# Two output panels of the first layer as seven half-size products each, with a longer six-slot stretch of the weight ring

## The chip, the cores and the metric

One core of one Trainium2 chip runs the whole program. The metric is the device time of that core in microseconds (us); lower is better. A profile is one execution, recorded from the first to the last instruction (its span).

## The reference, cut to what matters

A float32 model on 256 tokens of width 1024: two blocks of attention with a convolutional feed-forward network, then two layers (`for i in range(DEPTH)`) of the part that matters here. Its first layer works on 512 tokens (256 of x and 256 of a context), its last one on the 256 of x.

```python
def branch_merge(ya, yb, yc, gates, w_branch, w_out):
    ga, gb, gc = jnp.split(jax.nn.sigmoid(gates), N_BRANCH, axis=-1)
    m = ga * (ya @ w_branch[0]) + gb * (yb @ w_branch[1]) + gc * (yc @ w_branch[2])
    return m @ w_out
...
        x = x + gt1 * branch_merge(ya, yb, yc, gates, w_branch[i], w_out[i])
...
            xc = xc + gt1c * branch_merge(yac, ybc, ycc, gatesc, w_branch[i], w_out[i])
        h2 = modulate(rmsnorm(x, g_norm2[i]), sh2, sc2)
        x = x + gt2 * ec_moe(h2, w_router[i], w_e1[i], w_e3[i], w_e2[i])
```

`ec_moe` sends each token through a router and then 16 experts, each with three matrices of 1024 x 1024 (4 MB each). All weights are read from HBM once, 664 MB in all.

## The kernel before, in words

**Tiling.** Activations are kept transposed: feature on the 128 partitions, token along the row. A weight panel is 512 output columns of a matrix, two chunks of 1 MB (512 rows x 512 columns each); `w_branch` has one chunk to a panel. `tiles_T` (L530) multiplies a panel directly: four tiles of 128 outputs, each with 8 matmuls (4 for `w_branch`) over all 512 tokens. Each float32 matmul stands as two records in the trace, so a direct panel of the first layer is 64 records of 512 columns. The sum of a tile lies in one of eight PSUM banks; VectorE (DVE) or ScalarE (ACT) empties it, and TensorE (PE) waits for a bank only when it comes round again (`Banks`).

**Half-size products.** `products` (L579) multiplies a panel by 512 tokens in another way: the panel and the tokens are cut in halves along rows, columns and tokens, and seven products p1 to p7 of half-size blocks take the place of eight. Each product is 8 matmuls (16 records) of 256 tokens. DVE forms three sums of token halves (T1_H, T2_H, T4_H, in `half_tokens`) and a fourth in place (`context_half`) once for all panels that share their tokens, and for each panel four sums of weight blocks (`prepare`: part 0 makes three, part 1 the fourth). PE waits for part 0 ahead of p6 and for part 1 ahead of p3. ACT copies p6 and p2 out of PSUM (`product_copy`), DVE adds the other five to them (`assemble`). The first layer's gate panels are already done so; the output panels (`w_out`) are direct.

**Order at the end of the first layer's mixing.** PE: gate panel (7 products), `w_branch` (direct), last gate panel, last `w_branch`, `shift_rows` (4 small matmuls), two direct output panels with `turn_tokens_half(0)` (16 transposes) after their fifth tile, the router's matmul (L1188), `turn_tokens_half(1)`, the router's steps between PE, ACT and DVE with three panels of modulation weights (`w_ada`, `ada_part`, L704), the gathering of tokens (L1235) and the experts (L1285). DVE: `merge_tile` (L2047, with one addition over four tiles, L2057, after each panel), then `add_gated` (L1736), which adds gate times output to the residual X.

**The ring.** One queue, SyncE's (SP), loads all chunks in the order in which PE uses them, into a ring of nine slots of 1 MB. The sums of tokens and weights lie in the last three (6 to 8). So `weight_chunks` marks stretches (`narrow`) in which only slots 0 to 5 may be used, and `slot_plan` gives each chunk the slot used longest ago among those allowed. A chunk waits at the head of the queue until its slot's last chunk has been used; one that takes back a slot of the sums waits for the last product of the stretch (`sums_done`, L1378). All behind it waits too.

**Loads aside.** Nine expert chunks of the first layer go to dead parts of the arena and of H, not to the ring: five when the attention is done, three when the gates are done, one when the output panels are done. `early` says ahead of which chunk of the queue each group is issued.

**The last layer's start.** PE: a panel for U (direct), two `ada_part`, a panel for V (two tiles, L571), two folds (L720), four transposes (L993), then products. DVE: four copies of U, two copies of V, `half_tokens`, `context_half`, `prepare` parts 0 and 1.

Of the kernel before, what the change touches and what calls it, by code (L numbers as in the profile page):

```python
# [21 lines left out]
KT = D // P  # L22
S = 256
# [156 lines left out]
def weight_chunks(a):  # L180
# [93 lines left out]
def build(nc, a, out, dump=None, stop=None):  # L274
    from contextlib import ExitStack
    ctx = ExitStack()
    with ctx:
# [175 lines left out]
        KT3, QT3, V3 = UT, VG, TG  # L453
        YCU = Y2[2]
        MBS = (view(0, 8, 512), view(0, 8, S))
        GS = [view(o, 4, 512) for o in (12288, 18432)]
# [51 lines left out]
        def _(pe):  # L508
# [69 lines left out]

            def products(rows=False):  # L579

# [3 lines left out]
                def product(name):  # L584
                    if name == PRODUCTS[0]:
# [5 lines left out]
                        panel.update(p1=(low[:, :, 0:S], H[:, 0:4, 0:S]), p2=(high[:, :, 0:S], H[:, 4:8, 0:S]),  # L591
                                     p3=(S4_W, H[:, 4:8, S:2 * S]), p4=(high[:, :, S:2 * S], T4_H),
                                     p5=(low[:, :, S:2 * S], T1_H), p6=(S2_W, T2_H), p7=(S3_W, H[:, 0:4, S:2 * S]))
                    if name in ("p6", "p3"):
                        pe.wait_ge(sums_ready.sem, sums_ready.nth("pe"))
                    w, t = panel[name]
                    o = banks.open("a" if name in ("p6", "p2") else "v")
# [6 lines left out]
                    ins.then_inc(banks.filled, 1)  # L604
                    turned_panels[-1][3][name] = sum(r[-1] == "a" for r in banks.uses)
                    if name in ("p5", "p4"):
# [3 lines left out]

                return [lambda name=name: product(name) for name in PRODUCTS]

# [345 lines left out]
            for i in range(DEPTH):  # L958
# [151 lines left out]

                def read_by(who):
                    return sum(r[-1] == who for r in banks.uses)

                def turn_mods():
# [59 lines left out]
                for f, step in enumerate(out_tiles):  # L1174
                    step()
                    written.append(read_by("v"))
                    if f == 4:
                        pe.wait_ge(banks.freed["v"], written[3])
                        turn_tokens_half(0)
# [4 lines left out]
                for s in range(qtiles // 2):  # L1184
                    for k in range(KT):
                        if s == 0 and (k % 4 == 0 or k == KT - 1):
                            pe.wait_ge(banks.freed["v"], written[min(k + 3, KT - 2) if k < KT - 1 else k])
                        ins = mm(o[32 * (k % 4):32 * (k % 4) + 32, s * S:(s + 1) * S], WRS[:, s, k, :], X[:, k, s * S:(s + 1) * S],  # L1188
# [208 lines left out]
        def _(v):  # L1397
# [375 lines left out]
            def context_half():  # L1773

                ve.tensor_tensor(H[:, 0:4, S:2 * S], H[:, 4:8, S:2 * S], H[:, 0:4, S:2 * S], ALU.subtract
                                 ).then_inc(half_sums.sem, half_sums.up())

            def part_of(dst, rows, f, t):

# [38 lines left out]
            for i in range(DEPTH):  # L1818
# [241 lines left out]
                def gate_sums(n):  # L2060

                    def last_part():
                        assemble("p4", GS[n % 2], more=n < 5)
# [3 lines left out]
                    return [lambda name=name: assemble(name, GS[n % 2], more=n < 5) for name in PRODUCTS[:-1]] + [last_part]  # L2067

# [32 lines left out]
                for half in range(2):  # L2101
                    if half and not last:
                        for step in gate_sums(5):
                            step()
                    for f in range(4):
                        merge_tile(4 + half, f)
                    stamp().then_inc(merged_ready.sem, merged_ready.up())
                o = banks.take("v")
# [3 lines left out]
                add_gated(i, 0, ns)  # L2112
                v.wait_ge(ssq_ready.sem, ssq_ready.nth("v"))
# [155 lines left out]
        def _(sc):  # L2269
# [179 lines left out]
            for i in range(DEPTH):  # L2449
# [138 lines left out]
                else:  # L2588
# [3 lines left out]
                    gate(GS[1])  # L2592
                table(LOG_EXP)

                def token_squares(t, half, o):
# [166 lines left out]
```

## Time and profile before

| | us |
|---|---|
| median of 3 runs | 2804.08 (2800.76 to 2805.63) |
| the profiled execution's own time | 2802.52 |
| its span | 2800.7 |
| PE busy in the span | 2551.8 (91%) |
| DVE busy | 948.9 (34%) |
| ACT busy | 464.7 (17%) |
| mean granted TensorE clock | 0.952 of full |

In a row of the trace, "1369.80 15.86 PE L550 ... x32 [5.19 <-DMA ring]" reads: 32 instructions of line 550 start at 1369.80 us, are over 15.86 us later, and PE had been idle for 5.19 us before them, until a transfer into `ring` landed. PEld is the loading of PE's stationary operand, SPq the DMA queue of SP, with the time at which a transfer was issued. The granted clock is 1.00 at 2.4 GHz and 0.50 at 1.2 GHz. Matmul records overlap, so the pace of a group is its time over its count.

### The profile page before, as it was taken

The numbers are of one execution on the slowest core, as the hardware profiler recorded it, in microseconds if no ns is written. First come the engines' busy times: TensorE is split into PE (matmuls) and PEld (weight loads), VectorE is DVE, ScalarE is ACT, GpSimd is POOL, SyncE is SP. The second block draws the span as 40 slices with busy tenths as digits, with TensorE's granted clock in tenths as the row PEclk, the third lists the DMA queues.
The fourth block names the chain that finished last, engine by engine and source line by source line (L and its number), as shares of the span: only waits on it lengthen the run. The fifth ranks groups of instructions, "written<-read, shape, count | busy, mean of one in ns | idle before, by whom it ended". The sixth has DMA issues, their size and how long they took to land.

```text
span 2800.7 us, 33063 instructions
## 1 busy us (share of the span) xinstructions
PE 2551.8 (91%) x14215; PEld 1721.2 (61%) x14215; DVE 948.9 (34%) x1929; ACT 464.7 (17%) x1019; POOL 60.5 (2%) x91
## 2 busy tenths in 40 slices
PE   8999999999999999999999998888999998666675
PEld 5678888568887877767554343334688885332322
DVE  2535501345514876554221121111574322110101
ACT  1320001141102132232021111113121211100001
POOL 1010000000000100000000000000100000000000
PEclk9999999999999999999999999999999999777767
DMA  8676444384444311210569999999414378999997
GB/s 306 221 191 179 156 155 155 120 271 150 151 150 138 113 61 61 75 61 31 195 241 378 414 421 421 421 421 346 128 61 166 105 287 341 421 421 421 420 421 293
DMA packets 202981, 664.42 MB, mean 237 GB/s; under 512 B 14226, under 2 KB 60596, under 8 KB 153940
## 3 DMA queue, kind: packets, MB, share of 16 engines
q1 hardware_dynamic: 193952, 641.97, 59.9%
q0 software_dynamic: 8688, 20.28, 2.8%
q8 instruction: 113, 1.85, 0.3%
q14 instruction: 32, 0.26, 0.0%
q10 hardware_dynamic: 196, 0.06, 0.0%
HBM read 661.12 MB, written 9.57 MB: 239 GB/s over the span
## 4 chain that ended last, share of the span: by engine, by line
PE 74%; DMA 21%; DVE 3%; ACT 2%; issue 1%; ACTq 0%; DVEq 0%
PE ps L550 29%; DMA ring<-in_w_e 20%; PE ps L603 15%; PE ps L1285 9%; PE ps L812 5%; PE ps L571 3%; PE ps L1262 1%; PE ps L1235 1%; PE ps L784 1%; PE ps L704 1%; PE ps L1084 1%; PE ps L1036 1%; PE ps L1049 1%; PE ps L1106 1%; PE ps L1024 1%
## 5 line engine op out<-in xcount | busy, mean ns | idle before, releaser
L1285 PE MATMUL ps<-ring,arena 128*32 128x256 f32 (+1 forms) x4344 | 588.1, 527 | 179.0 <-DMA ring<-in_w_e 171.3
L550 PE MATMUL ps<-normed,ring 128*128 128x256 f32 x2624 | 580.6, 382 | 5.1 <-ACT normed L2323 2.5
L550 PEld LDWEIGHTS ps<-normed,ring 128*128 128x128 f32 x2624 | 498.9, 191 | 80.2 <-ACT normed L2323 5.5
L1285 PEld LDWEIGHTS ps<-ring,arena 128*32 128x32 f32 (+1 forms) x4344 | 193.8, 133 | 553.1 <-DMA ring<-in_w_e 259.6
L550 PE MATMUL ps<-arena,ring 128*128 128x256 f32 (+1 forms) x832 | 255.8, 465 | 6.5 <-DMA ring<-in_w_branch 5.2
L550 PEld LDWEIGHTS ps<-arena,ring 128*128 128x128 f32 x832 | 156.8, 191 | 93.9 <-issue 73.3
L603 PE MATMUL ps<-ring 128*128 128x256 f32 x816 | 186.3, 382 | 2.7 <-DVE ring L1752 2.7
L603 PEld LDWEIGHTS ps<-ring 128*128 128x128 f32 x816 | 155.1, 192 | 27.3 <-issue 6.7
L603 PE MATMUL ps<-normed,ring 128*128 128x256 f32 x768 | 171.6, 380 | 0.1
L603 PEld LDWEIGHTS ps<-normed,ring 128*128 128x128 f32 x768 | 144.4, 190 | 21.3 <-issue 1.7
L812 PE MATMUL ps<-arena,ring 128*128 128x256 f32 x704 | 152.3, 379 | 0.0
L812 PEld LDWEIGHTS ps<-arena,ring 128*128 128x128 f32 x704 | 133.8, 190 | 18.2
L2231 DVE SCALAR_TENSOR_TENSOR arena<-arena,ps 128x512 f32<-128x512 f32 (+1 forms) x32 | 17.7, 554 | 366.6 <-ACT arena L2642 366.6
L1500 DVE TENSOR_TENSOR arena<-ps,small 128x256 f32<-128x256 f32 x128 | 52.0, 423 | 258.3 <-PE ps L550 209.7
L2650 ACT ACTIVATE normed<-ps 32x256 f32<-32x256 f32 (+1 forms) x96 | 42.7, 445 | 533.1 <-PE ps L1285 532.3
L1736 DVE SCALAR_TENSOR_TENSOR residual<-ps,small,residual 128x256 f32<-128x256 f32 x120 | 53.0, 481 | 186.4 <-PE ps L1262 115.1
L2236 DVE SCALAR_TENSOR_TENSOR arena<-arena,ps 128x512 f32<-128x512 f32 (+1 forms) x32 | 17.7, 554 | 233.1 <-PE ps L1285 233.1
L2345 ACT ACTIVATE arena<-arena 128x512 f32<-128x512 f32 (+2 forms) x32 | 31.2, 976 | 391.0 <-DVE arena L1581 267.4
L1494 DVE COPY arena<-ps 128x256 f32<-128x256 f32 (+1 forms) x58 | 25.9, 450 | 200.9 <-PE ps L812 129.7
L571 PE MATMUL ps<-ring,normed 128*128 128x512 f32 x192 | 83.7, 594 | 0.0
L2423 ACT ACTIVATE arena<-arena,small 128x512 f32<-128x512 f32 (+3 forms) x64 | 43.1, 674 | 236.6 <-DVE small L1706 124.2
L603 PE MATMUL ps<-ring,normed 128*128 128x256 f32 x320 | 71.4, 379 | 0.0
(288 smaller groups left out, 2229.4 us busy)
## 6 DMA issues: line engine op xcount, KB each, us to landing
ring<-in_w_e SPq DMA_DIRECT2D x363, 1024.0 KB, 20.3
ring<-in_w_in SPq DMA_DIRECT2D x56, 1024.0 KB, 5.3
ring<-in_w_ada SPq DMA_DIRECT2D x48, 1024.0 KB, 7.7
ring<-in_ffn_w_up SPq DMA_DIRECT2D x88, 512.0 KB, 6.4
ring<-in_ffn_w_down SPq DMA_DIRECT2D x22, 1024.0 KB, 5.4
ring<-in_dil_w_qkv SPq DMA_DIRECT2D x18, 1024.0 KB, 5.0
arena<-in_w_e SPq DMA_DIRECT2D x16, 1024.0 KB, 14.0
ring<-in_sb_w_qkv SPq DMA_DIRECT2D x12, 1024.0 KB, 14.9
```

The lines of the kernel that those rows point to most:

```text
L550: ins = mm(o[:, 0:n], slots[k // 4][:, k % 4, f * P:(f + 1) * P], src[:, k, 0:n], start=k == 0, stop=k == kts - 1)
L571: ins = mm(o, src[:, k, t * P:(t + 1) * P], slots[k // 4][:, k % 4, :], start=k == 0, stop=k == KT - 1)
L603: ins = mm(o[:, j * S:(j + 1) * S], still[:, k, j * P:(j + 1) * P], moving[:, k, :], start=k == 0, stop=k == 3)
L704: ins = mm(o[32 * (k % 4):32 * (k % 4) + 32, :], silu_pad[:, k, :], slots[k // 4][:, k % 4, :], start=k < 4, stop=k >= 4)
L784: ins = mm(outs[f][:, t:t + S], slots[k // 4][:, k % 4, f * P:(f + 1) * P], H[:, k, t:t + S], start=k == 0, stop=k == KT - 1)
L812: ins = mm(outs[f][:, 0:S], slot[:, k, f * P:(f + 1) * P], HID[:, 2 * j + k, :], start=j == 0 and k == 0, stop=j == FT // 2 - 1 and k == 1)
L1285: ins = mm(o[w * g:w * g + w, 0:cols], lhs(2 * c + j), part, start=c == 0 and j == 0, stop=c == KT // 2 - 1 and j == 1)
L1500: ve.tensor_tensor(dst, o[:, 0:S], rstd[:, 0:S], ALU.mult).then_inc(banks.freed["v"], banks.free("v"))
L1736: ins = ve.scalar_tensor_tensor(X[:, f, t], o[:, t], gt[:, f, s:s + 1], X[:, f, t], ALU.mult, ALU.add)
L2345: se.activation(x, x if src is None else src, ACT.Tanh, scale=scale).then_inc(gate_exp.sem, gate_exp.up())
L2423: return se.activation(s, s if src is None else src, ACT.Exp, bias=nmax[:, n % 2, k:k + 1], scale=scale, accum_out=ssum[:, n % 2, k:k + 1])
L2650: ins = se.activation(YE[q][r:r + CAP, (e - 1) // 4, g * cols:(g + 1) * cols], o[g * w + q * CAP:g * w + (q + 1) * CAP, 0:cols], ACT.Copy)
```

## The change

1. The two output panels of the first layer become seven products each, in the order p1, p2, p6, p7, p5, p3, p4, with sums of the merged tokens (`merged_sums`: four DVE subtractions). DVE adds each product straight to the residual (`add_products`), over two scratch areas to which ACT copies p2 and p6. The last output tiles' waits of the router's matmul are moved with it, and it takes the context half first.
2. `prepare` for the first output panel runs inside the last gate panel, for the second inside the first output panel.
3. The first layer's six-slot stretch ends behind the router's modulation panels instead of inside the last gates (chunks are numbered in the order of use: it ended at 165, now at 176). The eight loads aside go together ahead of chunk 170.
4. In the last layer, `half_tokens` and `context_half` come before the two copies of V instead of behind them.

```diff
+OUT_PRODUCTS = ("p1", "p2", "p6", "p7", "p5", "p3", "p4")
@@ weight_chunks
                 panel(w, 8 * BRANCH + b * D + half * BRANCH)
-                if i == 0 and b == MERGE_ORDER[2] and half:
-                    narrow[i] = (narrow[i], len(out))
                 panel(a["w_branch_2"][i][b], half * BRANCH, BRANCH)
         for half in range(2):
             panel(a["w_out_2"][i], half * BRANCH)
         ada_panels(ADA_ROUTER[i])
+        if i == 0:
+            narrow[i] = (narrow[i], len(out))
...
-        early[gates + 11], early[gates + 13] = held[:ASIDE_FIRST[i]], held[ASIDE_FIRST[i]:then]
+        if i == 0:
+            early[gates + 10] = held[:then]
+        else:
+            early[gates + 11], early[gates + 13] = held[:ASIDE_FIRST[i]], held[ASIDE_FIRST[i]:then]
@@ build, tensor
                 else:
                     gemm_products()
-                    sums_done.append(state["summed"])
...
-                out_tiles = tiles_T(MBS[i], qtok, halves=merged_ready) + tiles_T(MBS[i], qtok)
+                    out_products = (products(src=MBS[i], order=OUT_PRODUCTS,
+                                             before={"p1": merged_ready, "p2": merged_ready, "p6": half_sums, "p7": half_sums, "p4": half_sums})
+                                    + products(src=MBS[i], order=OUT_PRODUCTS))
+                    for n, step in enumerate(out_products):
+                        step()
+                        written.append(read_by("v"))
+                        if n == 9:
+                            pe.wait_ge(banks.freed["v"], written[6])
+                            turn_tokens_half(0)
+                    sums_done.append(state["summed"])
+                    x_written = {(1, 0): written[12], (0, 6): written[13]}
@@ build, vector
+            def merged_sums(part):
+                m = MBS[0]
+                if part == 0:
+                    ve.tensor_tensor(T1_H, m[:, 0:4, S:2 * S], m[:, 0:4, 0:S], ALU.subtract).then_inc(v_step.sem, v_step.up())
+                    return
+                v.wait_ge(v_step.sem, v_step.made)
+                ve.tensor_tensor(T2_H, m[:, 4:8, S:2 * S], T1_H, ALU.subtract).then_inc(half_sums.sem, half_sums.up())
+                ve.tensor_tensor(m[:, 0:4, S:2 * S], m[:, 4:8, S:2 * S], m[:, 0:4, S:2 * S], ALU.subtract
+                                 ).then_inc(half_sums.sem, half_sums.up())
+                v.wait_ge(half_sums.sem, half_sums.made)
+                ve.tensor_tensor(T4_H, T2_H, m[:, 4:8, 0:S], ALU.subtract).then_inc(half_sums.sem, half_sums.up())
...
+                o = product("p1")
+                v.wait_ge(banks.freed["a"], turned_panels[panels_read[0]][3]["p6"])
+                ve.tensor_tensor(c11, c11, o, ALU.add).then_inc(v_step.sem, v_step.up())
+                ve.tensor_tensor(c12, c12, o, ALU.add).then_inc(banks.freed["v"], banks.free("v"))
+                v.wait_ge(v_step.sem, v_step.made)
+                add(0, 0, c11)
+                o = product("p7")
...
                 if last:
+                    half_tokens(i)
+                    context_half()
                     for t in range(qtiles):
                         evac(VG[:, t, :], 512)
-                    half_tokens(i)
-                    context_half()
```

In `add_products` each `add` is two operations of the form of L1736 (128x256); p1 has two additions of 128x512 and one `add`, p7 one addition, `prepare(0, 1)` and one `add`, p5 two additions and two `add`, p3 one `add` and `prepare(1, 1)`, p4 one `add`. The second panel has no `prepare`.

## Rows read from the trace of the kernel before

**Rows 1.** The page: busy shares, and DMA's share of 40 slices of the span.

```profile
PE 2551.8 (91%) x14215; PEld 1721.2 (61%) x14215; DVE 948.9 (34%) x1929; ACT 464.7 (17%) x1019; POOL 60.5 (2%) x91
...
DMA  8676444384444311210569999999414378999997
```

**Rows 2.** Chain that ended last, 1300 to 2350 us: start, duration, what, instructions.

```profile
1326.70 13.73 PE ps L550 x32
1340.43 24.19 PE ps L603 x112
1364.64 5.11 DMA ring<-in_w_branch
1369.80 15.86 PE ps L550 x32
1386.00 34.43 PE ps L550 x80
...
1422.18 20.60 PE ps L550 x48
...
1885.39 20.32 DMA ring<-in_w_e
```

**Rows 3.** SP's queue in order of time: the first layer's output and router loads.

```profile
1364.64 0.37 SPq L1389 DMA_DIRECT2D ring<-in_w_branch  x1
1365.05 3.67 SPq L1389 DMA_DIRECT2D ring<-in_w_out  x4
```

**Rows 4.** Stretches: busy by engine, clock, DMA share, GB/s.

```profile
1360.00:1365.00 5.00, 4.61 (x22) 3.71 (x20) 1.04 (x2) 0.00 (x0) 0.00 (x0) 1.00 0.00 0
1370.00:1380.00 10.00, 10.00 (x20) 4.35 (x21) 1.38 (x2) 0.00 (x0) 0.00 (x0) 0.82 1.05 388
1470.00:1475.00 5.00, 3.54 (x26) 2.48 (x26) 4.05 (x12) 0.00 (x0) 0.00 (x0) 1.00 0.01 3
1700.00:1800.00 100.00, 89.74 (x428) 36.35 (x428) 17.20 (x39) 11.70 (x20) 0.00 (x0) 1.00 1.01 421
```

**Rows 5.** PE in order of time: third modulation panel, start of the first layer's experts.

```profile
1454.33 1.92 PE L704 MATMUL ps<-ring,small 128*32 128x512 f32 x16
...
1473.51 13.95 PE L1285 MATMUL ps<-ring,arena 128*64 128x512 f32 x64 [1.46 <-DVE arena L2201]
```

**Rows 6.** Groups by line and shape, 1298 to 1443 us.

```profile
L1736 DVE SCALAR_TENSOR_TENSOR residual<-ps,small,residual 128x256 f32<-128x256 f32 x15 | 6.6, 479 | 47.7 <-PE ps L550 47.7
L1792 DVE TENSOR_TENSOR arena<-arena,ps 128x512 f32<-128x512 f32 x2 | 1.4, 690 | 12.3 <-PE ps L603 12.3
L1748 DVE TENSOR_TENSOR ring<-ring 128x1024 f32<-128x1024 f32 x1 | 1.2, 1218 | 0.0
L2473 ACT ACTIVATE arena<-ps 128x512 f32<-128x512 f32 x4 | 2.4, 597 | 36.1 <-PE ps L603 36.1
```

**Rows 7.** DVE in order of time: the last merge of the first layer.

```profile
1385.69 0.69 DVE L2047 SCALAR_TENSOR_TENSOR arena<-arena,ps 128x512 f32<-128x512 f32 x1 [2.75 <-PE ps L550]
1386.41 2.29 DVE L2057 TENSOR_TENSOR arena<-arena 128x2048 f32<-128x2048 f32 x1
```

**Rows 8.** PE, then DVE, in order of time: the last layer's start.

```profile
1977.98 1.87 PE L720 MATMUL ps<-constants,arena 128*128 128x32 f32 x16
1983.77 1.09 PE L993 MATMUL ps<-constants,arena 128*128 128x128 f32 x4 [3.92 <-DVE normed L1775]
1987.57 5.57 PE L603 MATMUL ps<-ring 128*128 128x256 f32 x16 [2.72 <-DVE ring L1752]
2003.34 3.62 PE L603 MATMUL ps<-ring 128*128 128x256 f32 x16
...
1978.80 1.22 DVE L1767 TENSOR_TENSOR ring<-normed 128x1024 f32<-128x1024 f32 x1
1983.58 1.22 DVE L1748 TENSOR_TENSOR ring<-ring 128x1024 f32<-128x1024 f32 x1
```

**Rows 9.** Stretch at the start of the last layer, columns as in rows 4.

```profile
1980.00:1985.00 5.00, 1.09 (x4) 0.71 (x4) 4.90 (x6) 0.00 (x0) 0.00 (x0) 0.61 1.02 389
```

More of the change, by code:

```diff
@@ L454, in build @@
         YCU = Y2[2]
+        OUT_SUMS = (view(6144, 4, 512), view(18432, 4, 512))
         MBS = (view(0, 8, 512), view(0, 8, S))
@@ L577, in tiles_N, with read_by, products @@
                 return [lambda t=t: tile(t) for t in range(tiles)]
-            def products(rows=False):
+            def read_by(who):
+                return sum(r[-1] == who for r in banks.uses)
+            def products(rows=False, src=H, order=PRODUCTS, before={}):
                 panel = {}
                 def product(name):
-                    if name == PRODUCTS[0]:
+                    if name == order[0]:
                         taken = next_chunks(2)
@@ L604, in product @@
                     ins.then_inc(banks.filled, 1)
-                    turned_panels[-1][3][name] = sum(r[-1] == "a" for r in banks.uses)
+                    turned_panels[-1][3][name] = read_by("a")
                     if name in ("p5", "p4"):
@@ L609, in product @@
                         state["summed"] = len(banks.uses)
-                return [lambda name=name: product(name) for name in PRODUCTS]
+                return [lambda name=name: product(name) for name in order]
             def gemm_products(rows=False):
@@ L1109, in _ @@
                 staged(len(items), (0, da_scores), (2 * LAG, da_pv), (LAG, da_turn), fill=merge_tiles[gate_steps:])
-                def read_by(who):
-                    return sum(r[-1] == who for r in banks.uses)
                 def turn_mods():
@@ L1171, in _ @@
                 shift_rows()
-                out_tiles = tiles_T(MBS[i], qtok, halves=merged_ready) + tiles_T(MBS[i], qtok)
                 written = []
[L1174 to L1179, printed above, removed]
+                if last:
+                    out_tiles = tiles_T(MBS[i], qtok, halves=merged_ready) + tiles_T(MBS[i], qtok)
+                    for f, step in enumerate(out_tiles):
+                        step()
+                        written.append(read_by("v"))
+                        if f == 4:
+                            pe.wait_ge(banks.freed["v"], written[3])
+                            turn_tokens_half(0)
+                    x_written = {(0, 0): written[3], (0, 4): written[6], (0, 7): written[7]}
+                else:
+                    out_products = (products(src=MBS[i], order=OUT_PRODUCTS,
+                                             before={"p1": merged_ready, "p2": merged_ready, "p6": half_sums, "p7": half_sums, "p4": half_sums})
+                                    + products(src=MBS[i], order=OUT_PRODUCTS))
+                    for n, step in enumerate(out_products):
+                        step()
+                        written.append(read_by("v"))
+                        if n == 9:
+                            pe.wait_ge(banks.freed["v"], written[6])
+                            turn_tokens_half(0)
+                    sums_done.append(state["summed"])
+                    x_written = {(1, 0): written[12], (0, 6): written[13]}
                 out_done.append(len(banks.uses))
@@ L1183, in _ @@
                 pe.wait_ge(*banks.due)
-                for s in range(qtiles // 2):
+                for s in reversed(range(qtiles // 2)):
                     for k in range(KT):
-                        if s == 0 and (k % 4 == 0 or k == KT - 1):
-                            pe.wait_ge(banks.freed["v"], written[min(k + 3, KT - 2) if k < KT - 1 else k])
+                        if (s, k) in x_written:
+                            pe.wait_ge(banks.freed["v"], x_written[s, k])
                         ins = mm(o[32 * (k % 4):32 * (k % 4) + 32, s * S:(s + 1) * S], WRS[:, s, k, :], X[:, k, s * S:(s + 1) * S],
@@ new lines, in add_products, with add, product @@
+            def add_products(panel, more):
+                dst, f0 = OUT_SUMS[panel], 4 * panel
+                c11, c12, c21, c22 = (part_of(dst, False, f, t) for f in (0, 1) for t in (0, 1))
+                gt = mods[0][:, 16:24, :]
+                def add(f, t, src, g=gt):
+                    for j in range(2):
+                        n = f0 + 2 * f + j
+                        x = X[:, n, t * S:(t + 1) * S]
+                        ins = ve.scalar_tensor_tensor(x, src[:, j, :], g[:, n, t:t + 1], x, ALU.mult, ALU.add)
+                    return ins
+                def product(name):
+                    o = banks.take("v").rearrange("p (j n) -> p j n", j=2)
+                    v.wait_ge(banks.filled, banks.at["v"])
+                    return o
+                o = product("p1")
[5 more added lines that the diff above has]
+                o = product("p7")
+                v.wait_ge(banks.freed["v"], banks.frees["v"])
+                ve.tensor_tensor(c21, c12, o, ALU.add).then_inc(banks.freed["v"], banks.free("v"))
+                if more:
+                    prepare(0, 1)
+                v.wait_ge(banks.freed["v"], banks.frees["v"])
+                add(1, 0, c21).then_inc(v_step.sem, v_step.up())
+                o = product("p5")
+                ve.tensor_tensor(c22, c21, o, ALU.add).then_inc(v_step.sem, v_step.up())
+                ve.tensor_tensor(c12, c12, o, ALU.add).then_inc(banks.freed["v"], banks.free("v"))
+                v.wait_ge(v_step.sem, v_step.made)
+                add(1, 1, c22)
+                v.wait_ge(banks.freed["v"], banks.frees["v"])
+                add(0, 1, c12).then_inc(v_step.sem, v_step.up())
+                o = product("p3")
+                v.wait_ge(v_step.sem, v_step.made)
+                add(0, 1, o).then_inc(banks.freed["v"], banks.free("v"))
+                if more:
+                    prepare(1, 1)
+                o = product("p4")
+                add(1, 0, o, ampl).then_inc(banks.freed["v"], banks.free("v"))
+                panels_read[0] += 1
@@ L2062, in last_part @@
                     def last_part():
-                        assemble("p4", GS[n % 2], more=n < 5)
+                        assemble("p4", GS[n % 2])
                         v.wait_ge(banks.freed["v"], banks.frees["v"])
                         stamp().then_inc(gate_ready.sem, gate_ready.up())
-                    return [lambda name=name: assemble(name, GS[n % 2], more=n < 5) for name in PRODUCTS[:-1]] + [last_part]
+                    return [lambda name=name: assemble(name, GS[n % 2]) for name in PRODUCTS[:-1]] + [last_part]
                 gate_turn = [lambda: None] * 4
@@ L2104, in _ @@
                             step()
+                        merged_sums(0)
+                        ve.tensor_scalar(ampl, mods[0][:, 16:24, :], -1.0, None, ALU.mult).then_inc(v_step.sem, v_step.up())
                     for f in range(4):
@@ L2107, in _ @@
                     stamp().then_inc(merged_ready.sem, merged_ready.up())
+                    if not last and half:
+                        merged_sums(1)
                 o = banks.take("v")
@@ L2111, in _ @@
                                ).then_inc(banks.freed["v"], banks.free("v"))
-                add_gated(i, 0, ns)
+                if last:
+                    add_gated(i, 0, ns)
+                else:
+                    add_products(0, True)
+                    add_products(1, False)
+                    v.wait_ge(banks.freed["v"], banks.frees["v"])
                 v.wait_ge(ssq_ready.sem, ssq_ready.nth("v"))
@@ L2593, in _ @@
                 table(LOG_EXP)
+                if not last:
+                    for dst in OUT_SUMS:
+                        for name in ("p2", "p6"):
+                            product_copy(name, dst)
                 def token_squares(t, half, o):
```

8 lines of the change are left out of this document (5 added, 3 removed).

## The prediction

> **What bounds the kernel now.** I read the page first. PE is busy 91% of the span [rows 1], so a change that takes matmuls away can be worth their time, if PE is what sets the end where they stand. DMA's line has two stretches of nines: the experts of the two layers. There the chain of waits is made of transfers: each expert of the first layer ends in a wait like the 20.32 us one at 1885.39 [rows 2], while DMA runs at share 1.01 and 421 GB/s [rows 4]. So three kinds of stretch have to be told apart: where PE has work without a gap (the mixing), where DMA does (the experts), and the joint between them.
>
> The second view is the chain around the change [rows 2]. A gate panel of seven products is 24.19 us for 112 records, 3.46 us to a product. Then PE waits 5.11 us for the last `w_branch` chunk, and the two output panels take 34.43 + 20.60 = 55.03 us for 128 records. The queue says why it waits: that chunk is issued at 1364.64, when the last gate product ends, with all output chunks behind it [rows 3], and DMA had been idle until then (share 0.00 from 1360 to 1365, [rows 4]). It is a wait for a slot, not for bandwidth. It costs twice: the clock is at a mean of 0.82 from 1370 to 1380 [rows 4], and the `w_branch` panel behind the gap takes 15.86 us where its like took 13.73 [rows 2].
>
> The third is the joint. The first expert matmul starts at 1473.51 and was released by DVE, not by a transfer [rows 5]; DMA stands still from 1470 to 1475 (share 0.01, [rows 4]). So the ring is full before PE starts on the experts, and the stream of transfers restarts with the first chunk that PE frees. After that it is saturated, and what is left to move is the same. The experts of the first layer thus end earlier by as much as PE starts them earlier. All behind them follows from there, since the last layer's mixing follows PE too.
>
> **Part 1, the ring.** By the slot rule chunk 165 (the last `w_branch`) was the first to take back a slot of the sums, with 166 and 167. Now it takes the slot of chunk 159, used before the last two gate panels. PE goes on at 1340.43 + 24.19 = 1364.62. Gone are 5.11 us of waiting and 15.86 - 13.73 = 2.13 us of slow clock: **7.2 us**. What is late next? Chunk 167 waits for p4 of the gate panel before the last, done by 1326.70; with 5.1 us from issue to landing (1364.64 to 1369.80, [rows 2, 3]) it is there at 1332, and `prepare` for the first output panel wants it after p7 of the last gate panel, at 1354. Chunk 169 waits for p5 of that panel (1340.43 + 5 x 3.46 = 1357.7), lands at 1363, and is wanted at 1392. Both have over 20 us to spare. The eight loads aside are issued from 1358 and 1365, 8 x 2.5 us (1.05 MB at 421 GB/s) at the soonest; nothing wants them before the experts. Modulation chunks 170 to 173 wait for slots that come free by the end of the first output panel. Chunk 175 waits for the last output product; the third modulation panel is used 1454.33 - 1442.78 = 11.6 us after that [rows 2, 5], against 5.1 us of landing. SP has only this queue; POOL's is not touched.
>
> **Part 2, the products.** 2 x 24.19 = 48.4 us take the place of 55.03: **6.6 us** less. What they need beside PE: (a) DVE's four token sums, 4 x 1.22 = 4.9 us (form of L1748, [rows 6]). The first stands in the last gate panel's shadow. The merge ends at 1386.41 + 2.29 = 1388.70, 3.0 us after the last `w_branch` tile (1369.80 + 15.86 = 1385.66) [rows 2, 7], and a stamp more. The new order needs it for p2 only, which starts 0.34 us (`shift_rows`, 1385.66 to 1386.00) + 3.46 us behind that tile: covered, by some 0.6 us. This is the thinnest cover in the change; without it, it costs what it is short. The other sums are ready 4.4, 5.6 and 6.9 us behind the tile, p6, p7 and p4 start at 7.3, 10.7 and 24.5. (b) DVE's work on a panel: additions of 0.69, pairs of residual additions of 2 x 0.48 [rows 6]; p1 2.3, p7 1.7, p5 3.3, p3 and p4 1.0 each, with `prepare` 4.9: 14.1 us in the first panel, 9.2 in the second, under 24.2 of PE. A product's bank is wanted again eight openings later. `prepare` after p7 is over 3.7 us later, with p6 of the next panel still 18 us away. (c) ACT copies four products at 0.60 us [rows 6], with nothing else to do. (d) At the end the router's matmul starts on the context half and needs p4's additions (1.0 us) for its last two blocks only; before, it needed the last tile's two likewise. The queue of DVE behind its new waits holds only work for later products. I take the hidden parts at nothing.
>
> Both parts: 1386.00 is reached 7.3 us earlier, the outputs end 13.9 us earlier, near 1428.9.
>
> **Through the joint.** Behind the outputs the ring now has to take 11 chunks (175 to 183, 185 and the ninth load aside) before it waits for PE: 11 x 2.5 = 27.4 us. PE's first expert matmul stands 1473.51 - 1442.78 = 30.7 us behind the outputs, and its first freed chunk 1.7 us later (8 records of 13.95/64). So DMA still stands still for some 5 us, where it stood about twice that, and the 13.9 us pass.
>
> **Part 3, the last layer.** PE waits 3.92 us for the in-place half and 2.72 us for `prepare` [rows 8]. The four operations put ahead of V's copies took DVE from 1978.80 to 1983.58, 4.8 us; DVE was idle during the V panel, and V's first copy may be late, since two banks of eight are in use. `prepare` can start at 1978.8, and the first product at 1987.57 - 4.8 = 1982.8. **4.8 us.** What is late next is `prepare` itself, some 2 us beyond the transposes. The slow first product (5.57 us against 3.62) I leave as it is: the clock had fallen by a mean of 0.61 from 1980 to 1985 [rows 9] with PE idle from 1979.85, so it was down from about 1981.1, ahead of 1982.8.
>
> **The sum.** 7.2 + 6.6 + 4.8 = 18.7 us, with rounding. The profiled execution took 2802.52 us, 1.6 below the median of 2804.08. 2802.5 - 18.7 = 2783.8; from the median it is 2785.4. I take the middle, **2784.6 us**.
>
> **The rivals.** *The clock stays up in the last layer.* The row for the forecast is the fall at about 1981.1, for the rival that PE's gap shrinks from 6.6 to some 2 us and begins later with the transposes. Gain 5.57 - 3.62 = 2.0 us more: 2782.6. The Trainium skill, "TensorE: Matmul & The Clock Gate", section "What's actually happening", says that the gate follows the array's recent activity; by that rule a short enough gap keeps full rate. The 5.11 us wait above, with its 2.13 us of loss, agrees; no row here has a gap of this kind and length in this place. *DMA takes one chunk back.* Before, chunk 176 could come during the output panels, now only behind them. If DMA had no idle time left at the joint, 2.5 us would come back: 2787.1. It decides if PE starts the experts under 27.4 us behind the outputs; against it stand the 30.7 us. *The stall moves.* A later chunk (an output chunk, or 175) takes the place of 165, with the same 5.1 + 2.1 us: 2791.8. Against it the margins above. *The first layer's gain ends at the joint*, because DMA, not PE, sets the experts' start: only 4.8 us remain, 2798.5, no change that can be told. Against it the share of 0.01 [rows 4]. *Slower: DVE's work stands between the products.* If PE waits for DVE after each product, through banks or through the residual, all of 14.1 + 9.2 + 4.9 = 28.2 us can be exposed: 28.2 - 18.7 = 9.5 us slower, 2812. It decides from 18.7 of the 28.2 on. For it: DVE runs strictly in order, and its waits for ACT's p6 copy hold all behind. Against it: the gate panels have the same waits and a pace of 3.46 us without a gap [rows 2].
>
> **How the numbers follow.** Forecast 0.56, clock 0.25, chunk 0.06, moved stall 0.06, ended at the joint 0.04, slower 0.03. A measurement can tell about 0.2% (5.6 us) from no change. Faster by more: 0.93; within: 0.04; slower: 0.03. The range holds the first three cases with the 2.4 us by which runs lie off their middle (2800.76 to 2805.63), and comes near the moved stall: 2780 to 2791.
>
> **What would show it.** In the profile after: no wait of L550 for `w_branch`, its issue long before 1364; fourteen products of 3.46 us from about 1378.7 with no idle time ahead of p2; DMA's idle stretch before the experts about halved and first expert matmul near 1459.6; in the last layer no wait for the in-place half, and the first product 14 + 4.8 us earlier, at half clock or not. Wrong would be: idle time ahead of output products, an expert start less than 13 us earlier, or waits for transfers in the first expert.

## The result, and the profile after

The changed kernel takes 2785.40 us in the median of 4 runs (2783.41 to 2788.04), the kernel before 2803.69 us (2800.76 to 2805.63). The ratio is 0.9936, 95% interval 0.9924 to 0.9949: 18.3 us less. In a second round of five runs, beside the repeated experiments, it took 2783.28 us (2780.64 to 2785.22), with a ratio of 0.9924 (0.9911 to 0.9938). The profiled execution took 2783.41 us, its span is 2781.6 us.

PE in order of time, of the changed kernel; L555 is `tiles_T` (L550 before), L613 the products, L1208 the router's matmul, L1305 the experts:

```profile
1341.29 3.62 PE L613 MATMUL ps<-ring 128*128 128x256 f32 x16
...
1365.46 13.90 PE L555 MATMUL ps<-arena,ring 128*128 128x512 f32 x32
1379.20 0.51 PE L1142 MATMUL ps<-constants,arena 128*128 128x16 f32 x4
1379.56 7.15 PE L613 MATMUL ps<-arena,ring 128*128 128x256 f32 x32
1386.55 3.62 PE L613 MATMUL ps<-ring 128*128 128x256 f32 x16
...
1426.29 3.62 PE L613 MATMUL ps<-ring 128*128 128x256 f32 x16
1429.83 1.93 PE L1208 MATMUL ps<-residual,arena 128*32 128x256 f32 x32
...
1460.30 13.95 PE L1305 MATMUL ps<-ring,arena 128*64 128x512 f32 x64 [1.46 <-DVE arena L2291]
```

No bracket of idle time stands between the gates and the router's matmul. The last `w_branch` panel follows the gate products at full pace (13.90 us; 15.86 in [rows 2]), and p1 and p2 run on as one group of 7.15 us. The first row says also that this execution was 0.86 us late already ahead of the change (1341.29 against 1340.43, [rows 2]); such offsets, up to some 3 us among the profiles of this study, have to be taken off before clock times are compared. Lengths of stretches are the better measure.

The queue of SP, changed kernel:

```profile
1299.36 0.37 SPq L1409 DMA_DIRECT2D ring<-in_w_branch  x1
1320.84 38.27 SPq L1409 DMA_DIRECT2D ring<-in_w_out  x4
1359.16 6.82 SPq L1393 DMA_DIRECT2D arena<-in_w_e  x6
1366.03 0.91 SPq L1393 DMA_DIRECT2D normed<-in_w_e  x2
1366.98 63.32 SPq L1409 DMA_DIRECT2D ring<-in_w_ada  x6
1430.34 1.67 SPq L1409 DMA_DIRECT2D ring<-in_w_e  x3
```

The `w_branch` chunk is issued at 1299, not 1365 as in [rows 3], the output chunks from 1321 on, and the experts' stream starts at 1430.34, right behind the last product. Stretches, with columns as in [rows 4]:

```profile
1455.00:1460.00 5.00, 3.83 (x33) 3.64 (x31) 3.86 (x12) 0.00 (x0) 0.00 (x0) 1.00 0.83 344
1460.00:1465.00 5.00, 4.70 (x22) 1.63 (x24) 1.56 (x5) 0.00 (x0) 0.00 (x0) 1.00 0.33 93
...
1680.00:1860.00 180.00, 158.34 (x730) 60.76 (x728) 27.56 (x60) 21.29 (x36) 0.00 (x0) 1.00 1.01 421
```

DMA's share is 0.83 and 0.33 in two stretches of 5 us, so it stands still for 0.85 + 3.35 = 4.2 us before the experts free their first chunk, and is saturated behind it. DVE, then PE, in order of time at the thin cover and at the last layer's start:

```profile
1380.12 2.29 DVE L2138 TENSOR_TENSOR arena<-arena 128x2048 f32<-128x2048 f32 x1
1382.44 0.15 DVE L1433 COPY small<-small 128x1 f32<-128x1 f32 x1
...
1390.90 0.69 DVE L1832 TENSOR_TENSOR arena<-arena,ps 128x512 f32<-128x512 f32 x1 [4.67 <-ACT arena L2563]
...
1960.65 0.68 DVE L1514 COPY arena<-ps 128x512 f32<-128x512 f32 x1
1965.71 0.69 DVE L1514 COPY arena<-ps 128x512 f32<-128x512 f32 x1 [4.38 <-PE ps L576]
1966.32 1.22 DVE L1768 TENSOR_TENSOR ring<-ring 128x1024 f32<-128x1024 f32 x1
...
1970.31 6.22 PE L613 MATMUL ps<-ring 128*128 128x256 f32 x16 [2.46 <-DVE ring L1772]
1976.37 10.52 PE L613 MATMUL ps<-normed,ring 128*128 128x256 f32 x48
```

The signal of the second merged half (L1433) is up at 1382.59; p2 starts at 1379.56 + 3.46 = 1383.0. DVE's wait of 4.67 us for ACT's copy holds nothing that PE needs. In the last layer the wait for the in-place half is gone, the one for `prepare` is 2.46 us, and the first product is still slow. A stretch there, columns as in [rows 4]:

```profile
1965.00:1970.00 5.00, 2.85 (x22) 2.29 (x20) 4.22 (x4) 0.00 (x0) 0.00 (x0) 0.86 0.65 199
```

A mean clock of 0.86 with PE's transposes over at 1967.86 means that the clock was down from about 1968.6, some 0.7 us into the wait.

### The profile page after: what moved, and what is told of

The parts are those of the page before. It is cut to its first block, busy times and chain, and to the rows that moved or that the text cites. A ratio compares the mean times of both kernels' runs of the same rounds, so it can differ in the third digit from the quotient of the medians.

```text
span 2781.6 us, 33305 instructions
## 1 busy us (share of the span) xinstructions
PE 2540.8 (91%) x14311; PEld 1736.9 (62%) x14311; DVE 972.2 (35%) x1960; ACT 467.5 (17%) x1023; POOL 60.6 (2%) x91
## 4 chain that ended last, share of the span: by engine, by line
PE 74%; DMA 21%; DVE 3%; ACT 2%; issue 1%; ACTq 0%; DVEq 0%
PE ps L555 28%; DMA ring<-in_w_e 21%; PE ps L613 16%; PE ps L1305 9%; PE ps L822 5%; PE ps L576 3%; PE ps L1255 1%; PE ps L1282 1%; PE ps L794 1%; PE ps L714 1%; PE ps L1094 1%; PE ps L1046 1%; PE ps L1059 1%; PE ps L1116 1%; PE ps L1034 1%; PE ps L730 1%
## 5 line engine op out<-in xcount | busy, mean ns | idle before, releaser
L1305 PE MATMUL ps<-ring,arena 128*32 128x256 f32 (+1 forms) x4344 | 589.8, 528 | 181.2 <-DMA ring<-in_w_e 173.3
L555 PE MATMUL ps<-normed,ring 128*128 128x256 f32 x2624 | 582.0, 383 | 3.7 <-ACT normed L2413 1.7
L555 PEld LDWEIGHTS ps<-normed,ring 128*128 128x128 f32 x2624 | 500.3, 192 | 79.0 <-issue 4.5
L1305 PEld LDWEIGHTS ps<-ring,arena 128*32 128x32 f32 (+1 forms) x4344 | 194.7, 133 | 557.2 <-DMA ring<-in_w_e 264.3
L613 PE MATMUL ps<-ring 128*128 128x256 f32 x912 | 208.7, 383 | 2.5 <-DVE ring L1772 2.5
L555 PE MATMUL ps<-arena,ring 128*128 128x256 f32 (+1 forms) x704 | 198.5, 438 | 1.3 <-DVE small L1433 1.3
L613 PEld LDWEIGHTS ps<-ring 128*128 128x128 f32 x912 | 173.8, 192 | 29.6 <-issue 6.3
L613 PE MATMUL ps<-normed,ring 128*128 128x256 f32 x768 | 171.6, 380 | 0.1
L555 PEld LDWEIGHTS ps<-arena,ring 128*128 128x128 f32 x704 | 131.9, 190 | 57.6 <-issue 42.7
L613 PEld LDWEIGHTS ps<-normed,ring 128*128 128x128 f32 x768 | 144.4, 190 | 21.3 <-issue 1.7
L822 PEld LDWEIGHTS ps<-arena,ring 128*128 128x128 f32 x704 | 133.8, 190 | 18.2
L1756 DVE SCALAR_TENSOR_TENSOR residual<-ps,small,residual 128x256 f32<-128x256 f32 x104 | 45.7, 481 | 136.7 <-PE ps L1282 113.0
L613 PE MATMUL ps<-ring,normed 128*128 128x256 f32 x320 | 71.4, 379 | 0.0
```

Source lines behind the costliest of these rows:

```text
L555: ins = mm(o[:, 0:n], slots[k // 4][:, k % 4, f * P:(f + 1) * P], src[:, k, 0:n], start=k == 0, stop=k == kts - 1)
L613: ins = mm(o[:, j * S:(j + 1) * S], still[:, k, j * P:(j + 1) * P], moving[:, k, :], start=k == 0, stop=k == 3)
L822: ins = mm(outs[f][:, 0:S], slot[:, k, f * P:(f + 1) * P], HID[:, 2 * j + k, :], start=j == 0 and k == 0, stop=j == FT // 2 - 1 and k == 1)
L1305: ins = mm(o[w * g:w * g + w, 0:cols], lhs(2 * c + j), part, start=c == 0 and j == 0, stop=c == KT // 2 - 1 and j == 1)
L1756: ins = ve.scalar_tensor_tensor(X[:, f, t], o[:, t], gt[:, f, s:s + 1], X[:, f, t], ALU.mult, ALU.add)
```

## The experiments

All are compared by their median, and by the lengths of stretches of their profiled executions:

| us | outputs | joint | experts | start of last layer | first product |
|---|---|---|---|---|---|
| before | 144.47 | 30.80 | 490.64 | 23.42 | 5.41 |
| changed | 130.57 | 30.47 | 491.37 | 18.64 | 6.06 |
| changed, second round | 130.57 | 30.44 | 491.54 | 18.63 | 6.05 |
| ring_only | 137.16 | 31.00 | 491.06 | 23.42 | 5.41 |
| order_only | 144.53 | 30.80 | 490.93 | 18.66 | 3.53 |
| no_order | 130.57 | 30.46 | 491.30 | 23.42 | 5.37 |
| no_order, again | 130.57 | 28.94 | 491.13 | 23.42 | 5.24 |
| early_prepare | 130.57 | 30.44 | 491.74 | 16.01 | 3.46 |
| early_prepare, again | 130.57 | 30.48 | 491.03 | 16.01 | 3.46 |
| short_stretch | 130.57 | 37.79 | 492.58 | 18.60 | 5.17 |
| extra_1mb | 130.57 | 30.36 | 490.76 | 18.63 | 6.11 |
| extra_4mb | 130.57 | 30.46 | 498.29 | 18.64 | 3.53 |
| late_merge | 136.83 | 30.45 | 491.69 | 18.63 | 6.06 |

Outputs: from the small matmuls ahead of the last two gate panels (L1122 before) to the router's matmul. Joint: to the first expert matmul. Experts: to the V panel of the last layer. Start: to its first product. The last column runs to the next product. Each number is the difference of two starts in PE's order of time.

### The parts alone

The ring's change alone, on the kernel before:

```diff
-                if i == 0 and b == MERGE_ORDER[2] and half:
-                    narrow[i] = (narrow[i], len(out))
...
         ada_panels(ADA_ROUTER[i])
+        if i == 0:
+            narrow[i] = (narrow[i], len(out))
...
+        if i == 0:
+            early[gates + 10] = held[:then]
+        else:
+            early[gates + 11], early[gates + 13] = held[:ASIDE_FIRST[i]], held[ASIDE_FIRST[i]:then]
```

> The kernel before with the ring's change alone: the six-slot stretch reaches to the router's modulation and the eight loads aside go together; output panels direct, last layer as before. By the prediction's part 1 the wait for the last w_branch chunk (5.1 us) and the slow clock behind it (2.1 us) go, nothing takes their place: 7.2 us under the kernel before, 2796.5 us. If the stall only moves to a later chunk, or DMA takes one chunk back at the joint, 0 to 4.7 us under it.

Measured: 2797.52 us, ratio 0.9979 (0.9970 to 0.9988), 11 runs, beside 2803.61 for the kernel before: 6.1 us less. Its outputs are 144.47 - 137.16 = 7.31 us shorter, with no wait and no slow panel (L553 is `tiles_T` here):

```profile
1366.39 13.90 PE L553 MATMUL ps<-arena,ring 128*128 128x512 f32 x32
```

The stall went and did not move; the median shows 1.2 us less of the gain than the stretch. The last layer's order alone, on the kernel before:

```diff
                 if last:
+                    half_tokens(i)
+                    context_half()
                     for t in range(qtiles):
                         evac(VG[:, t, :], 512)
-                    half_tokens(i)
-                    context_half()
```

> The kernel before with the last layer's token sums ahead of the copies of V, nothing else. Theory: DVE's four operations leave PE's path, 4.8 us less, 2798.9 us; the trace of after shows the clock down for 0.6 us more on the first product, so 4.2 is as likely. If the experts' transfers of the last layer set its end whatever PE does before them, no change.

Measured: 2798.90 us, ratio 0.9985 (0.9976 to 0.9994), 11 runs: 4.7 us less. In the profiled execution the start is 4.76 us shorter, and the clock did not fall:

```profile
1983.78 3.69 PE L603 MATMUL ps<-ring 128*128 128x256 f32 x16 [2.49 <-DVE ring L1752]
```

```profile
1980.00:1985.00 5.00, 2.51 (x18) 2.17 (x18) 4.90 (x8) 0.00 (x0) 0.00 (x0) 1.00 0.94 324
```

Behind the same wait of 2.5 us this product took 3.69 us, where in the changed kernel it took 6.22. With the faster product (5.41 - 3.53) this profile gains 4.76 + 1.88 = 6.6 us, and its execution (2796.22 us) is the second fastest of the eleven. So the median's 4.7 us does not show that the clock stayed up in the others. And the changed kernel with the same edit undone:

> The changed kernel with the last layer's order put back: ring and products alone. Theory: 4.2 to 4.8 us over the changed kernel, 2790 us; against ring_only it leaves the products, 6.6 us less. If the products gain nothing beyond PE's own time, or the parts hide each other, it lies with ring_only or with the changed kernel.

> Repeated: 2789 to 2790 us by the stretches, 2786.6 if something else in the changed kernel eats three microseconds of the last layer's gain.

> The changed kernel as it is, beside no_order and early_prepare on the same chip, to have the three compared in more runs: the first round of no_order stood 1.2 us over the changed kernel and early_prepare 8.1 under it, where the stretches of their traces say 4.1 over (4.8 less 0.6 of slow clock) and 5.2 under. If the stretches are right and the rest is the scatter of few runs (their traces differ by up to 3 us in the last 15 us, by the clock of the last scatter): 2785 to 2786 us. If the order of the last layer costs something elsewhere: 2783 or under.

Measured: no_order 2786.62 us (5 runs) and 2786.67 us (5 more; ratios 0.9941, 0.9928 to 0.9954, and 0.9940, 0.9928 to 0.9952). The changed kernel in the second round: 2783.28 us. So in the nine runs of one and the ten of the other (medians of all: 2784.63 and 2786.65) the order is worth 2.0 us, not the 4.1 that the stretches of the two profiled executions give (23.42 - 18.64, less 6.06 - 5.37).

Of the rest, 0.6 us is seen: in both profiles of the changed kernel the time from the last layer's router matmul to its experts is 24.31 us, where no_order has 23.70. Most of these 0.6 us lie in the 16 folds there (L730: 3.62 us at a clock of 0.50, and 3.18 in no_order, where the mean over them is 0.64), and 24.3 to 24.5 us stand in just the four profiles whose first product takes over 6 us, for a reason not known. Some 1.5 us stay open, about what medians of so few runs with a spread of 5 us leave uncertain: the first round alone gives 1.2 us for the order, the second, on one chip, 3.4. Both expectations that the stretches gave for the repeats, 2785 to 2786 us and 2789 to 2790, were missed by some 2 to 3 us, both to the low side.

Against ring_only, no_order leaves the products (and the sums that feed them): 137.16 - 130.57 = 6.59 us in the outputs, and 2797.52 - 2786.65 = 10.9 us in the medians.

That is 4 us more than the stretches give, and it comes in part from the end of the program. The last matmuls behind the last transfer, of the kernel before and of the changed one, PE in order of time:

```profile
2781.06 1.94 PE L1285 MATMUL ps<-ring,arena 128*32 128x256 f32 x16 [0.52 <-DMA ring<-in_w_e]
2784.64 6.40 PE L1262 MATMUL ps<-arena,normed 128*128 128x256 f32 x16 [1.65 <-ACT normed L2650]
```

```profile
2765.49 1.07 PE L1305 MATMUL ps<-ring,arena 128*32 128x256 f32 x16 [0.97 <-DMA ring<-in_w_e]
2768.21 3.72 PE L1282 MATMUL ps<-arena,normed 128*128 128x256 f32 x16 [1.65 <-ACT normed L2744]
```

The same 16 matmuls take 6.40 or 3.72 us, by the clock granted while they run: 0.50 from 2785.70 to 2788.20 before, 1.00 from 2769.10 to 2771.60 in the changed kernel. In the second profile of the changed kernel they took 5.10. No edit touches them. The clock at the last transfer does not decide it: ring_only had 1.00 there and still took 6.64 us for them. From the experts' start in the last layer to the end of the span it is 454.7 us before and 451.6 after. The other profiles lean the same way: 454.5 and 454.1 us in ring_only and order_only, the two others with direct output panels, and 451.1 to 452.7 in nine of the ten with products, but 454.3 in the tenth (extra_4mb). Between ring_only and no_order it is 3.2 us, most of the 4 us in question. No part of the change planned it. Why the clock there should favour the kernels with products, or whether it fell so by chance, stays open.

### The joint

One and four more transfers of 1 MB, from HBM to HBM and read by nobody, issued behind the outputs:

```diff
                 if r in slot_back:
                     sp.wait_ge(banks.filled, sums_done[slot_back[r]])
+                    if slot_back[r] == 0 and slot_of[r] == NSLOT - 1:
+                        for x in range(4):
+                            sp.dma_start(spare[x], a["w_e1_2"][1][x][0:2 * P, :].rearrange("(p j) n -> p (j n)", j=2)).then_inc(loads["spare"], 16)
```

> The changed kernel with one more transfer of 1 MB (between two places in HBM, read by nobody) issued behind the output panels, ahead of chunk 178. Theory of the joint: DMA idles about 4.2 us before PE frees the first expert chunk, so 2.5 us of it are hidden: no difference. Rival (the stream of transfers has no idle time that matters, each MB moved behind the outputs counts): 2.5 us slower.

> The same with four transfers of 1 MB, some 10 us of DMA. Theory of the joint: 10 - 4.2 = 5.8 us slower, 2791.2 us. Rival, each MB counts: 10 us slower, 2795.4 us. If DMA's stream did not set the experts' end: no difference.

Measured: 2784.92 us with one (ratio 0.9935, 0.9922 to 0.9948), no difference; 2790.89 us with four (0.9955, 0.9943 to 0.9967), 5.5 us more than the changed kernel's first median. With one, DMA's gap is shorter by what the transfer takes:

```profile
1455.00:1460.00 5.00, 4.36 (x38) 4.17 (x36) 3.52 (x11) 0.00 (x0) 0.00 (x0) 1.00 1.02 426
1460.00:1465.00 5.00, 4.18 (x20) 1.50 (x22) 2.08 (x7) 0.00 (x0) 0.00 (x0) 1.00 0.68 233
```

Its idle time is now about 1.6 us, and the experts' stretch is no longer (490.76). With four, that stretch is 498.29 - 491.37 = 6.9 us longer, less than the 10 us that the transfers take by the estimate and 1.1 more than the 5.8 expected; DMA's share drops to 0.71 from 1450 to 1455 behind the added transfers, 1.5 us of new idle time (with one, it drops to 0.69 from 1440 to 1445), for a reason not tested. In that execution 2.5 us came back at the first product, which ran at full clock. So the stream of transfers sets the experts' end, and most of the 4 us of idle time ahead of them can be filled free of cost: 2.5 us were.

### Where the six-slot stretch may end

```diff
+        if i == 0:
+            narrow[i] = (narrow[i], len(out))
         ada_panels(ADA_ROUTER[i])
-        if i == 0:
-            narrow[i] = (narrow[i], len(out))
```

> The changed kernel with the six-slot stretch ended in front of the router's modulation panels (at chunk 170, not 176). Chunks 170 to 172 then take back the slots of the sums, so they wait for the last output product (1429.7 in after). Theory: the moved stall. The second modulation chunk lands some 7.5 us behind the outputs, the fourth 12.5, where PE wants them at 4.7 and 6.5; the two ada parts end 5 to 6 us late, and the experts with them: 4 to 6 us slower than the changed kernel, 2790.5 us. Rival: the router's steps on DVE hide the loads, or the ring then starts the experts' chunks no later: no difference.

Measured: 2793.00 us, ratio 0.9962 (0.9950 to 0.9974), 7.6 us over the changed kernel's first median, where 4 to 6 were expected. The modulation panels now wait for the outputs, and PE for them (the queue of SP, then PE's order of time; "issue" means that the trace names no releaser):

```profile
1430.32 6.97 SPq L1409 DMA_DIRECT2D ring<-in_w_ada  x6
```

```profile
1438.31 3.64 PE L714 MATMUL ps<-ring,small 128*32 128x512 f32 x16 [3.46 <-issue]
1443.73 3.34 PE L714 MATMUL ps<-ring,small 128*32 128x512 f32 x16 [1.78 <-issue]
1449.14 1.92 PE L714 MATMUL ps<-ring,small 128*32 128x512 f32 x16 [0.94 <-issue]
```

The joint grows by 37.79 - 30.47 = 7.3 us. The first two waits are 5.2 us, and the slow clock behind them adds 3.1 (3.64 and 3.34 us for what takes 1.92); against them stands PE's own wait of 1.06 us for DVE behind these panels in the changed kernel, which is gone here. The third wait, 0.94 us, falls where PE waits for the router's steps anyway. This is the rival of the moved stall, made real: the stretch has to reach past the modulation panels, at least past the first of them. Ends between 170 and 176 were not tried.

### The thin cover

```diff
                     for f in range(4):
                         merge_tile(4 + half, f)
+                    if half and not last:
+                        for _ in range(4):
+                            v.wait_ge(v_step.sem, v_step.made)
+                            ve.tensor_tensor(T1_H, MBS[0][:, 0:4, S:2 * S], MBS[0][:, 0:4, 0:S], ALU.subtract).then_inc(v_step.sem, v_step.up())
                     stamp().then_inc(merged_ready.sem, merged_ready.up())
```

> The changed kernel with one token sum (128x1024, 1.25 us with its wait) repeated four times ahead of the signal that the second merged half is ready: 5.0 us more of DVE in front of p2 of the first output panel. By the trace of after the cover there is 0.4 us. Theory: PE waits 4.6 us ahead of p2, and the clock falls as behind the old wait (about 2 us more): 4.6 to 6.7 us slower, 2791.5 us. Rival, that such a delay is hidden by the products or at the joint: no difference.

Measured: 2789.03 us, ratio 0.9952 (0.9941 to 0.9964), 3.6 us over the changed kernel's first median and 4.4 over that of its nine runs. PE, then DVE, in order of time:

```profile
1378.71 3.70 PE L613 MATMUL ps<-arena,ring 128*128 128x256 f32 x16
1386.71 5.41 PE L613 MATMUL ps<-arena,ring 128*128 128x256 f32 x16 [4.31 <-DVE small L1433]
...
1381.59 5.00 DVE L2193 TENSOR_TENSOR ring<-arena 128x1024 f32<-128x1024 f32 x4
1386.51 0.15 DVE L1433 COPY small<-small 128x1 f32<-128x1 f32 x1
```

The bracket counts from the modelled end of p1, not from where p2 would have followed. p1 starts at 1378.71 here, so p2 was due at 1382.17 and starts 4.54 us late. The signal, 3.03 us behind p1's start in the changed kernel, is 7.95 us behind it here (its L1433 starts at 1386.51): 4.92 us later. So the cover was 4.92 - 4.54 = 0.4 us. The product behind it is slow by 1.8 us, and the outputs are 6.26 us longer. The medians show less than the stretch, within their scatter.

### A further step

DVE idles 4.38 us between the two copies of V, and PE then waits 2.46 us for `prepare`. So `prepare` too goes ahead of the copies, on the changed kernel:

```diff
                 if last:
                     half_tokens(i)
                     context_half()
+                    prepare(0, 0)
+                    prepare(1, 0)
                     for t in range(qtiles):
                         evac(VG[:, t, :], 512)
-                    prepare(0, 0)
-                    prepare(1, 0)
```

> The changed kernel with the weight sums of the first product panel of the last layer (prepare, both parts, 4.9 us of DVE) also ahead of the two copies of V. In the trace of after DVE idles 4.4 us between the two copies, and PE then waits 2.46 us for prepare and runs its first product at half clock (6.22 us for 3.62). Theory: both go, 5.1 us less, 2780.3 us. Rival 1: the panel's chunks have not landed so early, DVE stops at them and V's copies come late: no gain or slower by some us. Rival 2: the gap goes but the clock falls anyway behind the small matmuls of the folds: 2.5 us less.

> Repeated: 2780.3 us by the stretches (2.6 us of waiting, 2.6 of slow clock under the changed kernel), 2777.3 if the early preparation brings three microseconds elsewhere.

Measured: 2777.27 us (4 runs; ratio 0.9907, 0.9893 to 0.9921) and 2776.54 us (4 runs; 0.9901, 0.9888 to 0.9915), on the same chip as the changed kernel's 2783.28. It is the best kernel of the study, some 27 us under the one before. PE in order of time:

```profile
1969.29 0.63 PE L1003 MATMUL ps<-constants,arena 128*128 128x128 f32 x4
1969.76 3.62 PE L613 MATMUL ps<-ring 128*128 128x256 f32 x16
1973.22 10.52 PE L613 MATMUL ps<-normed,ring 128*128 128x256 f32 x48
```

There is no gap and no slow product, in both profiled executions. The stretches give 18.64 - 16.01 = 2.6 us and 6.06 - 3.46 = 2.6 us, as expected, and another 0.7 at the joint of the last layer; the medians give 6.7 (second round, one chip) to 8.1. So the medians were expected near 2780.3 us and are 3 to 4 us lower. Of that the 0.7 is seen; the rest stays open. Neither rival holds: the chunks had landed, and the clock stayed up.

## Why the prediction was right

**The number.** Forecast was 2784.6 us, measured 2785.40. The profiled execution ended 19.1 us earlier, where the sum said 18.7. By stretches it is 13.9 (outputs) + 0.3 (joint) - 0.7 (experts) + 4.8 (start of the last layer) - 0.65 (first product) - 0.6 (last layer's joint) + 3.1 (from there to the end), less the 1.0 us by which this execution was late at L1122. Two of these, the 3.1 at the end and the 1.0, are nothing that the sum foresaw; without them it would have been 17.0. So that the total lies within 1 us is in part luck: the parts of the change gave 1.7 us less in this profile than the 18.7, by slow clock and by the experts' stretch, and the end of the program gave more.

**Part 1, the ring** (7.2 us forecast): ring_only has 7.31 in the stretch and 6.1 in the median. Both halves of it, wait and slow clock, are gone; chunks 167, 169 and 175 had the time that was worked out (the last output chunk is issued at 1358.75, the last modulation chunk at 1429.93, and PE waits for neither). short_stretch shows what it costs where they have not.

**Part 2, the products** (6.6): 6.59 in the stretch. All hidden parts were hidden. The cover for p2 was put at 0.6 us; the rows show 0.4, and so does late_merge. One reading was wrong without effect: p4 was put at 24.5 us behind the last `w_branch` tile, which is the time of an eighth product. It is the seventh and starts 21.0 us behind the tile (at 1400.36), still long after its sum, ready at 6.9. The rival of DVE between the products fell: there are fourteen products without idle time. late_merge shows that DVE can be exposed there, but one for one behind the thin cover only.

**The joint** (13.9 pass through, some 5 us of DMA's idle time left): 4.2 us are left of 9.0 (DMA's shares before are 0.43, 0.01 and 0.77 in the stretches of 5 us from 1465 on), and the experts' start is 13.2 us earlier by the clock, 14.2 with the late start taken off. That the rest is real slack, and that the stream behind it is the bound, is shown by the two runs with transfers added. The rival of the one chunk, and the one that the gain ends at the joint, fell with them.

**Part 3, the last layer** (4.8): 4.78 in the profile, 4.7 in the medians of order_only, but 2.0 in those of the changed kernel against no_order. The 4.8 us are thus shown by the stretches; the medians bound them loosely.

**The clock rival** (0.25) was too narrow a question. I had the clock fall, at the time of [rows 9], or stay. Here it fell and stayed down through more of the first product (6.22 us; 5.57 in [rows 8]); in order_only and extra_4mb it stayed up behind the same wait. Of the seven profiles with this wait, four have 6.05 to 6.11 us from the first product to the next, both of the changed kernel among them; short_stretch has 5.17, and two have 3.53. The forecast's term, the slow product left as it was, was short by 0.65 us here. The Trainium skill, "TensorE: Matmul & The Clock Gate", section "What's actually happening", has the rate follow recent activity. With a gap of 2.5 us after small matmuls, these runs show both outcomes; early_prepare, which has no gap, is at full rate in both of its profiles.

## What to carry to other kernels

A wait for a transfer while DMA was idle was here a wait for a slot: in such a case see which chunk holds the place and where in the queue it stands, before bytes are counted. Between two stretches with different bounds, look at the joint: the loads stood still there, so a gain ahead of it passed in full, and the idle time said roughly how much could be loaded for nothing. When a small wait of PE is left behind another that was removed, look for the idle time of the engine that it waits for; the last 2.5 us here were worth twice that by the stretches, since the clock fell in them.

## What the runs showed beyond what was expected

The granted clock makes 2 to 3 us of difference in one place between kernels whose work there is the same: the first product of the last layer takes 3.53 to 6.11 us to its successor, the last 16 scatter matmuls 3.72 to 6.64. Two such places are as large as a part of this change, so sums of parts from medians of five runs, with a spread of 5 us, are good to some 2 us and no better; the outputs' stretch, which has no wait, repeats to 0.01 us (130.57 in all nine profiles with the products as they are), the experts' only to 1 or 2 us.

Slow clock cost nothing where PE had a wait behind it anyway. In the repeat of no_order the third modulation panel of the joint took 3.60 us instead of 1.92, ahead of a wait for DVE that shrank by as much (1.38 us, 3.05 in the others), and the folds behind it ran at full clock sooner (2.10 us to the gathering instead of 3.32). So that joint is the shortest, 28.94 us against 30.46.
